# Eight unused unit-matrix products become thirty-five unused products of the split input in seven forms, ahead of the second block's first norm

## The reference

```python
    # end of first_block, layer 1
    x = _layernorm(DEEPNORM_ALPHA * x + f + e, ln_ffn_g[i], ln_ffn_b[i])   # f: experts
    ...
    # start of second_block, layer 0
    h = rmsnorm(x, norm_mix_g[l])
    proj = h @ w_in[l]
```

## Time and profile before

| | us |
|---|---|
| three runs, median | 2648.48 |
| lowest and highest of them | 2642.61 and 2650.26 |
| span of the profiled execution, first to last instruction | 2645.5 |
| TensorE busy in it | 2556.8 |
| VectorE busy in it | 1269.3 |

### The profile page before, as it was taken

One profiled execution on the slowest core, in us unless ns is written; L12 is line 12 of the kernel. 1 busy time (PEld: TensorE's weight loads), 2 busy tenths in 40 slices (PEclk: granted clock), 3 DMA queues, 4 the chain that ended last, 5 costly groups with the idle time before them and its releaser, 6 DMA issues.

```text
span 2645.5 us, 66516 instructions
## 1 busy us (share of the span) xinstructions
PE 2556.8 (97%) x30782; PEld 2085.4 (79%) x30782; DVE 1269.3 (48%) x1710; ACT 942.9 (36%) x1227; POOL 173.9 (7%) x178
## 2 busy tenths in 40 slices
PE   8999999999999999999999999998999999989999
PEld 7977799897786767767667765687779978877997
DVE  6677655556861000010100101388467857846785
ACT  4455443355540000000000000266545645654663
POOL 1000000000000000000000000202500000160000
PEclk9999999999999999999999999999999999999999
DMA  6445855554459999999999999743035445313443
GB/s 218 142 160 174 307 179 182 152 191 161 149 180 394 407 396 404 412 405 409 398 404 410 405 398 418 287 155 117 31 120 185 171 166 194 105 51 121 171 173 104
DMA packets 94362, 635.37 MB, mean 240 GB/s; under 512 B 11328, under 2 KB 12256, under 8 KB 24320
## 3 DMA queue, kind: packets, MB, share of 16 engines
q1 hardware_dynamic: 85392, 598.61, 59.0%
q0 software_dynamic: 7120, 29.70, 4.0%
q10 hardware_dynamic: 1568, 2.75, 0.3%
HBM read 626.17 MB, written 13.24 MB: 242 GB/s over the span
## 4 chain that ended last, share of the span: by engine, by line
PE 79%; DVE 11%; ACT 5%; issue 3%; DMA 3%; SPq 0%; DVEq 0%; ACTq 0%
PE ps L1032 31%; PE ps L756 13%; PE ps L758 13%; PE ps L757 13%; DVE wlo L1946 3%; DMA raw<-in_units_dram 3%; ACT whi L1481 2%; PE ps L1331 1%; ACT s L1829 1%; PE ps L1310 1%; PE ps L1342 1%; DVE s L2306 0%; DVE mx L2268 0%; DVE x L2381 0%; PE ps L964 0%
## 5 line engine op out<-in xcount | busy, mean ns | idle before, releaser
L1946 DVE TENSOR_TENSOR wlo<-raw,whi 128x2048 fp32r<-128x2048 f32 (+5 forms) x250 | 531.6, 2135 | 306.5 <-ACT whi L1481 306.0
L1032 PE MATMUL ps<-raw,xe 128*32 128x256 f32 x10752 | 585.3, 379 | 5.5 <-DMA raw<-in_units_dram 4.7
L1032 PEld LDWEIGHTS ps<-raw,xe 128*32 128x32 f32 x10752 | 391.1, 110 | 194.5 <-DMA raw<-in_units_dram 7.0
L1481 ACT ACTIVATE whi<-raw 128x2048 fp32r<-128x2048 f32 (+4 forms) x252 | 447.8, 1780 | 203.7 <-PE ps L758 188.8
L756 PE MATMUL ps<-xTh,whi 128*128 128x256 f32 x1480 | 418.1, 283 | 0.0
L758 PE MATMUL ps<-xTh,wlo 128*128 128x256 f32 x1480 | 417.4, 282 | 0.0
L757 PE MATMUL ps<-xTl,whi 128*128 128x256 f32 x1480 | 417.3, 282 | 0.0
L2489 DVE TENSOR_TENSOR hb<-ps,hb 128x384 f32<-128x384 f32 x56 | 31.2, 558 | 777.5 <-ACT hb L1656 777.5
L1032 PE MATMUL ps<-raw,hTe 128*32 128x256 f32 x5376 | 291.8, 379 | 3.5 <-issue 3.5
L756 PEld LDWEIGHTS ps<-xTh,whi 128*128 128x128 f32 x1480 | 279.1, 189 | 0.8 <-issue 0.7
L757 PEld LDWEIGHTS ps<-xTl,whi 128*128 128x128 f32 x1480 | 278.8, 188 | 0.1
(11 more groups left out here) (582 smaller groups left out, 3229.7 us busy)
## 6 DMA issues: line engine op xcount, KB each, us to landing
raw<-in_units_dram SPq DMA_DIRECT2D x544, 1024.0 KB, 7.7
raw<-in_units_dram SPq DMA_DIRECT2D x18, 512.0 KB, 3.5
raw<-in_units_dram SPq DMA_DIRECT2D x6, 768.0 KB, 6.9
raw<-in_units_dram SPq DMA_DIRECT2D x8, 544.0 KB, 3.6
raw<-in_units_dram SPq DMA_DIRECT2D x6, 688.0 KB, 4.0
g<-in_b_gate_dram POOLq DMA_DIRECT2D x16, 256.0 KB, 9.2
raw<-in_units_dram SPq DMA_DIRECT2D x4, 576.0 KB, 4.5
rows_y<-yb ACTq DMA_DIRECT2D x7, 288.0 KB, 6.4
```

What stands on the lines that cost most here:

```text
L1032: ins = self.e.matmul(bands(ps[r:r + 32, 256 * i:256 * i + 256]), G.x[:, kk, o:o + 32], w[:, k, :, c:c + 128], start=(kk == 0 and i != 1), ...
L1481: self.e.activation(self.m.hi[u % NHL][:, 0:n], self.m.raw[u % NRAW][:, 0:n], ACT.Copy) \
L1946: self.e.tensor_tensor(self.m.lo[u % NHL][:, 0:n], self.m.raw[u % NRAW][:, 0:n], self.m.hi[u % NHL][:, 0:n].bitcast(F32), ALU.subtract) \
```

## The change

At the first norm of the second block, the number handed to `awake` goes from 8 to 5, and `awake` branches on it: below 5 it does what it did, so the other two places keep their three unit-matrix products. At 5 it issues five products in each of seven forms, 35 in all. All take 128 columns of `xTh` as the stationary operand, alternating between two of its eight blocks, and `xTh` as the moving one. The forms are, in order: 512 adjacent columns; 512 columns taken every second element; 128 columns read four times over; 512 columns taken in steps of 16 elements; 256 adjacent columns; 512 adjacent columns with 64 of the 128 rows; and 512 adjacent columns in one accumulation group over the five. Nobody reads the results.

```diff
-        self.awake(ps, {("n0", 0): 8, ("f20", 1): 3, ("f21", 1): 3}.get((tag, t), 0))
+        self.awake(ps, {("n0", 0): 5, ("f20", 1): 3, ("f21", 1): 3}.get((tag, t), 0))
...
     def awake(self, ps, n):
 
-        wide = self.m.ident[:, :].unsqueeze(1).broadcast_to([128, 4, 128])
-        for k in range(n):
-            self.e.matmul(ps[:, 0:512], self.m.ident[:, :], wide, start=True, stop=True)
+        if n < 5:
+            wide = self.m.ident[:, :].unsqueeze(1).broadcast_to([128, 4, 128])
+            for k in range(n):
+                self.e.matmul(ps[:, 0:512], self.m.ident[:, :], wide, start=True, stop=True)
+            return
+        x = self.m.xT[0]
+        flat = x[:, :, :].rearrange("p k n -> p (k n)")
+        one = flat[:, 0:512]
+        forms = [(ps[:, 0:512], one, ALL), (ps[:, 0:512], flat[:, 0:1024].rearrange("p (n a) -> p a n", a=2)[:, 0, :], ALL),
+                 (ps[:, 0:512], x[:, 0, 0:128].unsqueeze(1).broadcast_to([128, 4, 128]), ALL),
+                 (ps[:, 0:512], flat[:, 0:512].rearrange("p (a b) -> p b a", b=16), ALL), (ps[:, 0:256], flat[:, 0:256], ALL),
+                 (ps[:, 0:512], one, slice(0, 64))]
+        for out, moving, r in forms:
+            for j in range(n):
+                self.e.matmul(out, x[r, j % 2, 0:128], moving[r], start=True, stop=True)
+        for j in range(n):
+            self.e.matmul(ps[:, 0:512], x[:, j % 2, 0:128], one, start=(j == 0), stop=(j == n - 1))
```

## The result

The changed kernel takes 2653.53 us (median of 11 runs, 2649.96 to 2655.78), the kernel before 2647.47 us (11 runs, 2642.61 to 2650.98). The ratio is 1.0024, 95% interval [1.0017, 1.0032], so it is slower by 6.1 us. The forecast was no change, 2648.5 us, with a range up to 2654. The page after shows 38 instructions more, which are the 70 of the 35 new products (a weight load and a product each) less the 32 of the eight old ones (two passes each).

What follows compares the result with a forecast made beforehand. VectorE's chain through `hrm` bounds the seam, with TensorE idle 1.22 us: 7.65 us added for 6.87 removed puts 0.78 us into idle time, so 0.0 us change, 2648.5 us, range 2643.5 to 2654.

Steps and rivals of the forecast that it cites:

- no change that a measurement of this kernel tells: Outcome class for the whole kernel, holding the forecast itself, slow stepped forms and chance elsewhere; chance 0.90.
- The 7.9 us taken for what can be told: Whole kernel: 0.3% of its time, about what a measurement can tell from no change.
- What is removed: At the norm: eight plain two-pass products leave TensorE's queue, 16 x 0.429 = 6.87 us, worth nothing by itself.
- the adjacent forms: At the norm: new products reading adjacent columns cost 0.235 us each at 512 columns, 0.120 us at 256.
- The stepped forms at 0.235 us: At the norm: ten products with every second element or steps of 16 run at full rate, 2.35 us in all.
- the first rival: At the norm: one or both stepped forms slow, up to two passes' time, 0.5 to 5.6 us more; chance 0.30.
- The room of 8.33 us: Ahead of the transposes: break-even time for the 35 products, from 1692.24 until `hrm` arrives at 1700.57.
- the passing on of a delay: Behind the first tile's transposes: any lateness of the 35 products is passed on in full, 0.5 to 5.6 us in cases priced.
- the sum of 7.65 us: At the norm: time of all 35 new products, 30 x 0.235 + 5 x 0.120 us.
- Nothing of the change reaches there: Said of the later place where the clock falls at 1824: the change has no effect there.
- the fourth rival: Chance elsewhere puts the comparison of medians beyond 7.9 us on either side; chance 0.06, half on each side.
- The clock and VectorE's `x`: At the norm: granted clock stays 1.00 from 1692 to 1708, and VectorE's `x` still takes 5.1 us.

Runs made afterwards that it cites:

- e1: Changed kernel with its two stepped forms reading 512 adjacent columns instead: 2651.17 us, ratio 1.0014 to the kernel before.
- e4: Changed kernel with seven other forms: adjacent, steps of 2, 4, 8, 32, pairs, and a stepped stationary operand: 2654.65 us, ratio 1.0033 to the kernel before.
- e7: Kernel before with seven unit-matrix and 11 quarter-array products in place of eight unit-matrix ones, 40 instructions more: 2650.86 us, ratio 1.0017.
- e5: Kernel before with four unit-matrix and 68 quarter-array products in place of eight unit-matrix ones, 256 instructions more: 2645.99 us, ratio 0.9998.
- e8: Kernel before with seven unit-matrix and 65 quarter-array products in place of eight unit-matrix ones, 256 instructions more: 2648.36 us, ratio 1.0003.
- e12: Changed kernel plus one 256-column and 54 quarter-array products, 256 instructions more than the kernel before: 2651.05 us, ratio 1.0021 to the kernel before.
- e10: Kernel before with seven unit-matrix and 17 quarter-array products in place of eight unit-matrix ones, 64 instructions more: 2652.61 us, ratio 1.0021.
- e2: Kernel before with six unit-matrix and 29 64-column fp32r products in place of eight unit-matrix ones, 50 instructions more: 2650.68 us, ratio 1.0014.
- e9: Kernel before with five unit-matrix and 51 quarter-array products in place of eight unit-matrix ones, 192 instructions more: 2644.94 us, ratio 0.9997.
- e11: Kernel before with four unit-matrix and 60 quarter-array products in place of eight unit-matrix ones, 224 instructions more: 2647.10 us, ratio 1.0002.

## Why the prediction was right and where it failed

The number was within the range, and "no change that a measurement of this kernel tells" was the class with 0.90. That is partly luck. The range reaches to 2654 because both stepped forms were priced at two passes (5.6 us), and they cost 1.5 us of the path; 4.5 us came from a mechanism that the prediction doesn't have. The 7.9 us taken for what can be told was too coarse as well: eleven runs on each side tell 6 us. And the forecast stood on a median of three runs, 2648.5, where eleven give 2647.5. Point by point:

- **What is removed**, 6.87 us of queue, and **the adjacent forms**: right but for the switches named below. In e1 all 35 read adjacent columns, take 8.03 us where 7.65 were summed, and the seam is as before.
- **The stepped forms at 0.235 us**: wrong. They cost 0.45 and 0.43 us, so ten of them cost 4.4 us and not 2.35. I took the value of the nearest row and made slow stepped forms the first rival; the rival's mechanism was right. The half rate was priced for the steps of 16 alone, since by the Trainium skill, page "SBUF — State Buffer", section "Door 1: The DMA port swizzle (why `[64,N]` ≈ `[32,N]`)", every second element should be free. e4 shows that every step tried costs about the same.
- **The room of 8.33 us** and the passing on of a delay: right. The 35 take 10.12 us and the seam is 1.5 us later; 10.12 - 8.33 = 1.8 was to be expected, and 0.3 us of it is made up because `hrm` is complete by then: its eight transposes take 1.03 us and not 1.32. In the sum of 7.65 us the switches were missing too: around the five products on 64 rows, starts lie about 0.1 us further apart on four occasions (0.21 us where 0.12 is usual, and 0.34, 0.32 and 0.34 where 0.235 is), 0.4 us in all.
- **"Nothing of the change reaches there"**, said of the stages behind the seam in the fourth rival: this is the step that failed. 38 more instructions on TensorE reach all that lies behind them. In e1 and e7 that alone costs 3.5 and 3.7 us, and 256 more cost nothing that can be told (e5, e8). It is the larger part of the 6.1 us. The order of instructions showed the number 35 against 8, and I priced only their time.
- **The clock and VectorE's `x`**: as foreseen. The granted clock is 1.00 at the seam, and VectorE's two halves of `x` still span 5.2 us. Not foreseen: in the trace of the changed kernel the clock is 0.50 from 2395.96 to 2402.78, at the end of the second layer's delta stage, where it is 1.00 in the kernel before. The traces of e1, e7 and e12 are at 0.50 from about 2392 on too, for a few us. Over this stretch the changed kernel's delay grows from 5.5 us (2390) to 6.4 (2416), so what this clock costs is within 0.9 us.

What stays open: why the rest at +38 instructions is 4.5 us in the changed kernel, 3.5 in e1 and 1.6 in e4 (five runs). The intervals cover it, but something in the relative timing of engines could be part of it. That TensorE waits at the edges of pieces is shown by the place of the cuts, which moves with the number of instructions and comes back after 256. How the cuts make up the loss is not shown. Those of 0.25 us and more at the edges add up to 9.3 us in both delta stages before and to 10.7 in the changed kernel, 1.4 us more where 4.5 are lost, so what waits behind a cut must matter too. Why one cut lasts 0.5 and another 1.6 us was not tested.

## What to carry to other kernels

Count the instructions that an edit adds ahead of a stage of small products, and not only their time. Find waits on "issue" inside a group of like instructions, and see whether they move. If an edit there costs or gains a few us that no wait explains, pad it to the same place in the piece of 256 instructions before judging it. Where two kernels should differ at one place only, read the granted clock there in every run: in three of the twelve experiments it fell at the seam and made a delay that the products ahead hadn't made. A moving fp32r operand read in steps of 2 to 32 elements cost nearly double here, whatever the step; the stationary one, read every second element, cost nothing.

## What the runs showed of the hardware

- An fp32r product of 512 columns starts 0.235 us behind the one before if the moving operand is adjacent or repeated in runs of 128 elements, and 0.43 to 0.46 us behind it with steps of 2, 4, 8, 16 or 32 elements, or with pairs of adjacent elements two apart. The Trainium skill, page "SBUF — State Buffer", section "Door 1: The DMA port swizzle (why `[64,N]` ≈ `[32,N]`)", calls 32-bit steps up to 4 elements free; the measurement disagrees. For steps of 16 it has a penalty for each access to another line, and one is there: 0.43 us for 0.235, a factor of 1.8.
- Going from 128 rows to 64 and back cost about 0.2 us each time, in the changed kernel and in e1; on 64 rows the starts lie 0.23 to 0.24 us apart, as on 128.
- In the delta stages TensorE's program comes in packets of 16384 bytes about every 4 us, with almost no other traffic on the DMA engines. At many of the edges, 256 instructions apart, the engine stands still, for up to 1.7 us. In the kernel before, from 1890 to 1913 us, each packet starts 1.2 to 1.3 us behind an edge, and the next edge is passed 2.4 to 2.8 us behind the packet's start, so one piece follows the other every 3.6 to 4.0 us. The place of the edges is worth up to about 6 us of 2647 (e10, by its ratio 5.6).
- The granted clock fell to 0.50 behind the unread products in e2, e9 and e11, and that cost 0.7 to 1.1 us of the path; in the eleven other traces it stayed at 1.00 there.
